# Two transformer stacks on one core: order of the first loads, of blocks at a seam, and of ScalarE's table loads

## Time and profile before

| what | value |
|---|---|
| three executions | 2781.55, 2787.64, 2789.39 us; median 2787.64 |
| the profiled execution | 2785.67 us |
| its span, first to last instruction | 2783.9 us |
| TensorE busy | 2505.9 us, 90% of the span |
| VectorE, ScalarE, GpSimd busy | 1736.6, 970.3, 672.7 us |
| DMA | 803.18 MB, 289 GB/s over the span |

### The profile page before, as it was taken

One profiled execution on the slowest core, in us unless ns is written; L12 is line 12 of the kernel. 1 busy time (PEld: TensorE's weight loads), 2 busy tenths in 40 slices (PEclk: granted clock), 3 DMA queues, 4 the chain that ended last, 5 costly groups with the idle time before them and its releaser, 6 DMA issues. The chain is left out here.

```text
span 2783.9 us, 29395 instructions
## 1 busy us (share of the span) xinstructions
PE 2505.9 (90%) x9829; PEld 1558.4 (56%) x9829; DVE 1736.6 (62%) x3951; ACT 970.3 (35%) x2012; POOL 672.7 (24%) x636
## 2 busy tenths in 40 slices
PE   8989888798887899887877799999999999999999
PEld 3544444364442465442322357885688668865787
DVE  1678766755758656667776456654565546646664
ACT  1225322234222353222221135442444445424543
POOL 0044433433434333444444211002000020002000
PEclk9999999999999999999999999999999999999999
DMA  8399999999999999999999832544154315533452
GB/s 336 116 408 421 416 421 421 414 421 417 406 421 419 406 394 372 421 421 422 421 421 421 356 123 103 198 153 180 49 208 166 143 71 193 185 118 121 148 188 102
DMA packets 112849, 803.18 MB, mean 289 GB/s; under 512 B 13139, under 2 KB 15782, under 8 KB 20310
## 3 DMA queue, kind: packets, MB, share of 16 engines
q0 software_dynamic: 74464, 540.07, 47.2%
q1 hardware_dynamic: 38262, 261.60, 24.8%
HBM read 800.55 MB, written 4.22 MB: 289 GB/s over the span
## 5 line engine op out<-in xcount | busy, mean ns | idle before, releaser
L1345 PE MATMUL psum<-weights,scratch 128*128 128x512 f32 x1232 | 587.6, 622 | 144.8 <-ACT scratch L1778 144.8
L2762 POOL DMA_INDIRECT weights<-in_peer_uv,scratch x308 | 355.7, 1155 | 593.4 <-PE psum L1345 496.7
L1345 PEld LDWEIGHTS psum<-weights,scratch 128*128 128x128 f32 x1232 | 232.3, 197 | 468.9 <-issue 244.4
L1345 PE MATMUL psum<-arena,scratch 128*128 128x512 f32 x816 | 388.1, 621 | 76.2 <-ACT scratch L1778 76.1
L2606 DVE TENSOR_TENSOR piece<-weights,piece 128x2048 fp32r<-128x2048 f32 x128 | 292.0, 2292 | 181.5 <-ACT piece L1857 181.5
L1076 PE MATMUL psum<-weights,xT 128*128 128x512 f32 (+2 forms) x792 | 340.2, 584 | 20.9 <-DMA weights<-in_w_qkv_a 12.2
L1453 PE MATMUL psum<-piece,hidden 128*128 128x512 f32 x1536 | 358.9, 390 | 0.0
L1770 ACT ACTIVATE scratch<-scratch 128x2 f32<-128x2 f32 x256 | 51.9, 203 | 844.6 <-DVE heads_arena L2257 843.8
L1410 PE MATMUL psum<-split_x,piece 128*128 128x512 f32 x896 | 318.6, 398 | 0.0
L1453 PEld LDWEIGHTS psum<-piece,hidden 128*128 128x128 f32 x1536 | 284.3, 188 | 59.6
L1345 PEld LDWEIGHTS psum<-arena,scratch 128*128 128x128 f32 x816 | 154.0, 196 | 287.4 <-issue 163.2
(11 more groups left out here) (264 smaller groups left out, 2762.6 us busy)
## 6 DMA issues: line engine op xcount, KB each, us to landing
weights<-in_w_up SPq DMA_DIRECT2D x64, 1024.0 KB, 4.9
weights<-in_w_down SPq DMA_DIRECT2D x64, 1024.0 KB, 4.9
weights<-in_w_kv_b SPq DMA_DIRECT2D x16, 1024.0 KB
weights<-in_peer_w_q SPq DMA_DIRECT2D x12, 1024.0 KB
weights<-in_a_w_in SPq DMA_DIRECT2D x6, 2048.0 KB, 8.8
weights<-in_w_q_b SPq DMA_DIRECT2D x8, 1024.0 KB
weights<-in_w_o_b SPq DMA_DIRECT2D x8, 1024.0 KB
weights<-in_a_w_out SPq DMA_DIRECT2D x4, 2048.0 KB, 8.4
```

The source lines that it names most:

```text
L1345: mm = pe.matmul(psum[g.bank][:, :], diagonal[:, n % DIAGONALS, :], row[:, D + half * BANK:D + (half + 1) * BANK], start=(k == 0), stop=(k ...
L2762: pool.indirect_dma_start(gathered[n % GATHER_SLOTS], None, rows, bass.IndirectOffsetOnAxis(ap=expert[:, w % NT, k:k + 1], axis=0), elemen ...
```

## The change

Seven edits, all in the order of the lists:

1. SyncE issues chunks 1 and 2, `const`, chunks 3, 4 and 5, and only then the small broadcasts and the tiny loads. lambda's broadcast gets a semaphore of its own, and `consts_loaded` counts the other eight.
2. `gain_turn` and the bias row move behind `later_blocks[2]` on TensorE, and their copies behind `diff_out_turn` on ScalarE; they use banks 6 and 7.
3. VectorE's waits move: for lambda alone ahead of its product, for the other eight ahead of `sublayer_norm(0)`, for `bias_read` ahead of `angles`, for `bias_written` ahead of the first window.
4. On ScalarE the sine goes ahead of the copy of the first expert queries.
5. In the seam's `selected`, tile 0 is multiplied with chunk 2 ahead of tile 1's turn.
6. `exp_ahead`, an exponential of one column whose result nothing uses, goes ahead of the copy of the last input block in `selected`.
7. The same in `window`.

```diff
--- before.py
+++ after.py
@@ -78,7 +78,7 @@
 PIECES = 2 * FF // PIECE_FF
 SPLIT_SLOTS = 4
 
-CONSTS_LOADED = 16 * 9
+CONSTS_LOADED = 16 * 8
 SBUF_START = 16512
 
 
@@ -375,6 +375,7 @@
         first_loaded = [sem(f"first_loaded{n}") for n in range(FIRST_PARTS)]
         const_loaded = sem("const_loaded")
         consts_loaded = sem("consts_loaded")
+        lambda_loaded = sem("lambda_loaded")
         values_loaded = [sem(f"values_loaded{n}") for n in range(2)]
         high_heads_loaded = sem("high_heads_loaded")
         bias_written = sem("bias_written")
@@ -708,8 +709,6 @@
 
         diff_in0 = in_ready.plan(2 * NT)
         diff_blocks = [diff_block(0, n, n) for n in range(4)]
-        gain_turn = Turn([([norm_gains[0:GAIN_ROWS, :]], gainT[:, 0:GAIN_ROWS].rearrange("p (a b) -> p a b", a=1))], (4,))
-        bias_row_group = group(5)
         diff_blocks.append(diff_block(0, 4, 6))
         diff_turn = diff_turned(0, (2, 3, 4, 5))
         diff_blocks.append(diff_block(0, 5, 7))
@@ -717,6 +716,8 @@
 
 
         later_blocks = {2: diff_block(1, 2, 0)}
+        gain_turn = Turn([([norm_gains[0:GAIN_ROWS, :]], gainT[:, 0:GAIN_ROWS].rearrange("p (a b) -> p a b", a=1))], (6,))
+        bias_row_group = group(7)
         diff_out_turn = maps_turned(0, (4, 5))
         diff_out_chunks = [halved_chunk(A["w_o_a"][0], 0, high_heads, high_heads_loaded, 16, None),
                            in_weights(A["w_o_a"][0], 1, 2, later_blocks[2][-1])]
@@ -930,9 +931,9 @@
 
         @block.sync
         def _(sp):
-            def load_small(name, src):
+            def load_small(name, src, loaded=consts_loaded):
                 at, width = SMALL_COLS[name]
-                sp.dma_start(small[:, at:at + width], src.partition_broadcast(P)).then_inc(consts_loaded, 16)
+                sp.dma_start(small[:, at:at + width], src.partition_broadcast(P)).then_inc(loaded, 16)
 
             def load_chunks(chunks):
                 for c in chunks:
@@ -972,10 +973,10 @@
                 part = slice(n * KB // FIRST_PARTS, (n + 1) * KB // FIRST_PARTS)
                 sp.dma_start(xT[:, part, :], A["x_turned"][:, part, :]).then_inc(first_loaded[n], 16)
                 sp.dma_start(first.view[:, part, :], first.src[:, part, :]).then_inc(first_loaded[n], 16)
-            load_chunks(diff_chunks[1:2])
+            load_chunks(diff_chunks[1:3])
             sp.dma_start(const[:, :], A["const"]).then_inc(const_loaded, 16)
-            load_chunks(diff_chunks[2:3])
-            load_small("lambda_qk", A["lambda_qk_a"][0].rearrange("a d -> (a d)"))
+            load_chunks(diff_chunks[3:6])
+            load_small("lambda_qk", A["lambda_qk_a"][0].rearrange("a d -> (a d)"), lambda_loaded)
             load_small("subln_g", A["subln_g_a"][0])
             load_small("a_q_gain", A["a_q_gain"].rearrange("a d -> (a d)"))
             load_small("a_k_gain", A["a_k_gain"].rearrange("a d -> (a d)"))
@@ -984,7 +985,6 @@
             load_small("b_sinks", A["b_sinks"][0])
             load_small("c_q_gain", A["c_q_gain"][0])
             load_small("c_k_gain", A["c_k_gain"][0])
-            load_chunks(diff_chunks[3:4])
             gain_at = 0
             for src, rows in ((A["norm_mix"], 4 * KB), (A["norm_mlp"], 4 * KB), (A["c_q_a_gain"], 2), (A["c_kv_a_gain"], 1)):
                 sp.dma_start(norm_gains[gain_at:gain_at + rows, :],
@@ -993,7 +993,6 @@
             sp.dma_start(pos_i[:, :], A["positions"][0].rearrange("(t p) -> p t", p=P),
                          allow_slow_non_contiguous=True).then_inc(bias_read, 16)
             sp.dma_start(rel_bias[0:N_BUCKETS, :], A["rel_bias"]).then_inc(bias_read, 16)
-            load_chunks(diff_chunks[4:6])
             load_chunks(diff_out_chunks[0:1])
             sp.dma_start(x[:, :, :], A["x"][0].rearrange("(t p) d -> p t d", p=P)).then_inc(x_loaded, 16)
             load_ln(0)
@@ -1493,8 +1492,10 @@
 
             def selected(l):
                 project(l.in0[1] if l.n == 0 else l.in0[0], turned=l.x_turn[0].done)
+                if l.n == 0:
+                    project(l.in0[2])
                 turn_normed(l.x_turn[1], l.normed0 + 1)
-                for n in range(2 if l.n == 0 else 1, 4):
+                for n in range(3 if l.n == 0 else 1, 4):
                     project(l.in0[n])
                 project(l.in1[2], turned=l.x_turn[1].done)
                 pe.wait_ge(prepared.sem, l.k_ready[0] + 1)
@@ -1573,12 +1574,6 @@
             project(diff_blocks[0:1], in_parts=True)
             project(diff_blocks[1:4])
             pe.wait_ge(const_loaded, 16)
-            pe.wait_ge(bias_read, 16 * 6)
-            turns(gain_turn)
-            bank_free(bias_row_group)
-            pe.matmul(psum[bias_row_group.bank][0:HEADS, 0:384], rel_bias[0:N_BUCKETS, :],
-                      const_at("bucket_of")[0:N_BUCKETS, :], start=True, stop=True)\
-                .then_inc(psum_filled[bias_row_group.bank], 1)
             project(diff_blocks[4:5])
             pe.wait_ge(in_ready.sem, diff_in0 + 1)
             turns(diff_turn)
@@ -1589,6 +1584,12 @@
                 copied(block[-1])
             attend(diff, "diff", 0, HEADS)
             project([later_blocks[2]])
+            pe.wait_ge(bias_read, 16 * 6)
+            turns(gain_turn)
+            bank_free(bias_row_group)
+            pe.matmul(psum[bias_row_group.bank][0:HEADS, 0:384], rel_bias[0:N_BUCKETS, :],
+                      const_at("bucket_of")[0:N_BUCKETS, :], start=True, stop=True)\
+                .then_inc(psum_filled[bias_row_group.bank], 1)
             pe.wait_ge(in_ready.sem, diff_in0 + 2)
             turns(diff_out_turn)
             project(diff_out_blocks, turned=diff_out_turn.done)
@@ -1629,6 +1630,10 @@
             def root(k, n, at=0):
                 act.wait_ge(root_asked.sem, k + 1)
                 act.activation(root_out[:, at:at + n], root_in[:, at:at + n], ACT.Sqrt).then_inc(root_given, 1)
+
+            def exp_ahead():
+
+                act.activation(lam[:, 6:7], lam[:, 5:6], ACT.Exp)
 
             def exps(att, sink0=None, first=0, last=NT * HEADS):
                 for u in range(first, last):
@@ -1789,9 +1794,9 @@
                 root(ln_root[0, 0], 1)
                 outputs([later_blocks[3]], to_y)
                 turns(peer_turn)
-                queries(0)
                 act.wait_ge(angle_ready, 1)
                 act.activation(ang[:, :, 2, 0:ROPE], ang[:, :, 1, 0:ROPE], ACT.Sin).then_inc(sine_ready, 1)
+                queries(0)
                 scores_of(peer_scores[0:2], 0)
                 gate(0, 0)
                 outputs([later_blocks[n] for n in (4, 5)], to_y)
@@ -1909,10 +1914,6 @@
                 return y[:, t, at:at + w]
 
             outputs(diff_blocks[0:4], to_y)
-            turns(gain_turn)
-            filled(bias_row_group)
-            act.activation(scratch[0:HEADS, 0:384], psum[bias_row_group.bank][0:HEADS, 0:384], ACT.Copy, scale=HD ** 0.5)\
-                .then_inc(psum_freed[bias_row_group.bank], 1)
             outputs(diff_blocks[4:5], to_y)
             turns(diff_turn)
             act.wait_ge(lambda_asked, 1)
@@ -1922,6 +1923,10 @@
             root(diff_root[0], PEER_HEADS)
             outputs([later_blocks[2]], to_y)
             turns(diff_out_turn)
+            turns(gain_turn)
+            filled(bias_row_group)
+            act.activation(scratch[0:HEADS, 0:384], psum[bias_row_group.bank][0:HEADS, 0:384], ACT.Copy, scale=HD ** 0.5)\
+                .then_inc(psum_freed[bias_row_group.bank], 1)
             first_queries()
             experts()
 
@@ -1943,6 +1948,7 @@
                 turns(l.key_turn[1], None, 0, -1)
                 keys_apart(l.key_turn[1].groups[-1], 1, 2, 1)
                 relus(l.index[1])
+                exp_ahead()
                 outputs(l.in1[1], to_y)
                 exps(l.att, None, 0, HEADS)
                 turns(l.out_turn[0])
@@ -2417,12 +2424,14 @@
                     for _ in steps:
                         pass
 
+                dve.wait_ge(consts_loaded, CONSTS_LOADED)
                 whole(sublayer_norm(0))
                 rope(later_blocks[2])
                 dve.wait_ge(x_loaded, 16)
                 add_to_x(diff_out_blocks, ALPHA)
                 whole(layer_norm(0, 0))
                 rope(later_blocks[3])
+                dve.wait_ge(bias_read, 16 * 6)
                 angles()
                 dve.tensor_tensor(small_at("c_k_gain")[:, 0:NOPE], small_at("c_k_gain")[:, 0:NOPE], small_at("c_q_gain")[:, 0:NOPE], ALU.mult)
                 then(dve.tensor_scalar(neg_sink[:, :], small_at("b_sinks"), -1.0, None, ALU.mult))
@@ -2430,6 +2439,7 @@
                 whole(route(0, 1))
                 shares(0, 0)
                 shares(0, 1)
+                dve.wait_ge(bias_written, 16)
                 second_norm = sublayer_norm(second.t)
                 for w in range(WINDOWS):
                     for pair in range(PAIRS_IN_TILE):
@@ -2660,7 +2670,7 @@
             for block in diff_blocks[0:3]:
```

(4 more changed lines are left out.)

## The result

The changed kernel took **2762.75 us** (median of 5 runs, 2758.80 to 2764.89) against 2787.64 (5 runs, 2778.89 to 2790.41), a ratio of **0.9924** (95% interval 0.9908 to 0.994). The forecast had the sign right and the size too small: a gain of 13.9 against 24.9 between the two medians, and 2773 with a range down to 2767. The five runs of before lay high: the two medians alone would give 0.9911, and in three later groups of 23 to 29 runs the kernel before had medians of 2782.38 to 2784.34. The profiled execution after took 2758.8, its span is 2757.0, TensorE's mean granted clock is 0.985 (before 0.981).

The account below looks back on a forecast made before the run. No engine bounds all: TensorE bounds start-up and the dense layers, with expert-row gathering near 420 GB/s between. Gains 6.9 + 0 + 4.1 + 2.9 = 13.9 us off the profiled 2785.67 gave 2771.8, as a median 2773; range 2767 to 2782.

Parts of the forecast that it names:

- part 1: Start-up: all projection chunks ahead of the small loads, so the fourth block ends earlier; 6.0 us, bounds 4.0 to 6.3.
- part 5: Exponential's table loaded ahead of selected and window attention in layers 0, 1 and 3; 0.96 us each, 2.9 in all.
- Part 2: Start-up: gain transpose and bias row moved behind attention; 0.9 us off TensorE, hidden later in a wait of 1.16.
- Part 3: Sine first on ScalarE, ahead of the first routing; worth 0 to 0.8 us, taken as 0.
- Part 4: Seam: tile 0's third block ahead of tile 1's transposes, key transposes at 1613.6 against 1617.75; 4.1 us, bounds 0 to 4.3.
- The two covers: Seam: third block's weights in by 1594.2 against 1595.9 needed; VectorE's keys ready by 1611.9, 1.7 us ahead of TensorE.
- A: Rival, start-up: bias copies meet the second output chunk's load, ending it up to 2.5 us late; 2776 us; chance 0.14.
- B: Rival: covers at the seam or early table loads fail; gain 6.9 + 0 to 3, 2779 us; chance 0.11.
- D: Rival: front gains nothing, chunk 3 held up in SyncE's queue; gain 7 to 8, 2780 us; chance 0.08.
- C: Rival: gathering of expert rows loses rate, 14 us per 1%; 2797 us at 1.7%; chance 0.05.
- Chance or linked: Experiments' two theories: 1.2 GHz stretches on TensorE come and go between executions, or follow waits the change removes.

Follow-up runs that it names:

- bridge13: Kernel before plus two dummy matmuls ahead of the fourteenth head's transpose in window attention's first tile, filling the wait of 1.26 us; ratio 0.9985.
- bridge_front: Kernel before plus eight dummy matmuls between the start's third and fourth blocks, in the wait for chunk 3; order of loads kept; ratio 0.9998.
- after_bridge13: Changed kernel plus two dummy matmuls ahead of the fourteenth head's transpose in window attention's first tile; 2764.15 us, ratio 0.9919 of the kernel before.
- the three parts alone: Three kernels, each the kernel before with only the front, only the seam or only the early exponentials changed; ratios 0.9963, 0.9983 and 0.9975.
- loads_only: Kernel before with only the new load order, its semaphores and VectorE's waits; gain turn and bias row stay between fourth and fifth block; ratio 1.0007.
- same_after: The changed kernel unchanged, run again for a second profile; 2764.37 us, ratio 0.9923 of the kernel before.
- bridge: Kernel before plus two dummy matmuls in selected and window attention, where TensorE waits for the first exponential behind the table load; ratio 0.9987.

## Why the prediction was wrong in size

The sum failed in two terms: 6.0 for part 1 (measured 47.5 - 38.2 = 9.3), where blocks two and three were priced at a row that held a slow stretch, and 2.9 for part 5 (measured 7.4), where three waits were priced by their length without the clock behind them. The account by stages, from means over the profiles of the table that had a part and those that had not:

| part | forecast | measured |
|---|---|---|
| front (parts 1 and 2) | 6.9 | 156.35 - 146.15 = **10.2** |
| sine | 0 | 0 |
| seam | 4.1 | 28.08 - 24.26 = **3.8** |
| table, layer 0 | 0.96 | **1.1** |
| table, layer 1 | 0.96 | 294.82 - 291.91 = **2.9** |
| table, layer 3 | 0.96 | 305.98 - 302.56 = **3.4** |
| sum | 13.9 | **21.4** |

The old front's 156.35 is the mean of six profiles (before to bridge13 in the table), 146.15 that of five. Layer 0's is the time from the key transposes to its long run of matmuls: 254.7 to 254.8 without the early exponential and 253.6 to 253.8 with it, three profiles with a stretch at 1.2 GHz there left aside (bridge13 and bridge_front, behind the table's wait, and after_bridge13). 21.4 is within 0.3 of what the ratio gives, and the three parts alone gave 10.3 + 4.7 + 7.0 = 22.0 by their ratios: the parts add up.

**Part 1 failed** in the term of 6.0 (6.3 at most). It set the new end of the fourth block at 40.3 and the old at 46.57. The new end is 38.2 (mean of five). 1.8 of the 2.1 between came from taking blocks two and three at the 15.70 of the earlier trace rows. That row held a stretch at 1.2 GHz behind the first wait; at full clock it is 13.9, and the row, though it says so by its own length, was carried into the new kernel. Only two of eight profiles with the old order of loads showed that slow pair; in the other six it took 15.0, with a wait of some 0.87 for chunk 2 in it, which the new order also removes. The remaining 0.9 is the profile's: its fourth block ended at 46.57, in six profiles of that front on average at 47.5, since chunk 3's arrival and the clock behind the wait vary. The forecast put the clock into its lower bound (4.0 "if the clock still costs something") and not into its upper one, where two blocks at full clock would have stood.

**Part 2** was right: 0.9 taken out, 0.35 of cover left. What it missed is that it is the condition of part 1, as loads_only shows.

**Part 3** was right.

**Part 4** was right in mechanism and nearly in size. The wait is worth 27.19 - 24.26 = 2.9 (means of the four profiles of the old seam with full clock and of five of the new); the clock adds 1.6 in five of nine profiles. The profiled one was of these, and 4.5 there stands against 4.1. The two covers held: no wait for weights but one of 0.29 in after_bridge13, none for the keys.

**Part 5 failed** in pricing three waits by their length alone. By length they were right: 1.1, 0.98 (291.95 - 290.97) and 1.04 (303.60 - 302.56), together 3.1 against 2.9. The other 4.3 are stretches at 1.2 GHz that follow. The earlier trace rows had shown the pattern and I priced it at the seam, but did not look at the stretch behind the same kind of wait in layers 1 and 3, where the earlier trace rows stopped at the first exponential. In layer 3 a stretch is behind the table's wait in six of nine profiles, and in none of five with that wait filled or removed. Two more of the nine have theirs ahead of it, so the change can't have taken that one away: in the first pair of profiles 1.65 of layer 3's 2.69 was such luck, and in the means some 0.4 of the 4.3. In layer 1 all eight profiles with both waits had the stretch, two of four with the table's wait alone removed or filled, none of two with the 1.26 filled. So it seems to need the wait of 1.26, and the early exponential to lower its chance; with four and two profiles neither is certain.

The Trainium skill, "TensorE: Matmul & The Clock Gate", section "HAM oscillation — how this bites in real kernels", ties the lower clock to pauses of TensorE between bursts, in its case waits for a DMA of some 3 to 5 us. The traces agree for the pauses of 4 to 9 at the start; in the layers and at the seam the clock also fell behind pauses of 0.9 to 2.8, shorter than those of that section, and there not every time. The skill's "ScalarE: Activation LUTs", section "What ACT_TABLE_LOAD costs", would give 8.0 for this part by a drain beside the load, an estimate by its figure. The measured 7.4 looks like it and is not: the load is 1.28, the wait it made is worth 1.0 to 1.1 each time, and the rest is TensorE's clock.

**The rivals.** A did not happen: the second output chunk is issued earlier with the front (78.19) and took 9.1 to landing, so it was in by 87.3, and the copies started at 87.74. The two did not meet, here or in same_after (85.2 and 85.67), so what a meeting would cost stays open. The small margin is no luck: in all six profiles in which the bias rows were written while the chunk was under way they landed 0.2 behind it (87.44 behind 87.27 in after), and the copies wait for them. B and D are out (seam and front in the table). C, the gathering: 1427.5 to 1434.0 over all profiles, a mean of 1430.6 in the eight with the old order of the loads and of 1430.5 in the five with the full new front. The change does nothing to it, and of the 26.9 between the two profiled executions 5.5 is this spread (1433.6 and 1428.0). It does not go by TensorE's clock: after and same_after took 1428.0 and 1433.6 at granted clocks of 0.97 and 0.98, with the DMA engines busy all the time (share 1.00) at 413 and 411 GB/s. What decides the rate was not tried.

**Chance or linked** ends between the two: at the start, the seam and in the layers each stretch at 1.2 GHz has a wait at or just ahead of it, and with that wait it comes in all profiles (the wait for chunk 3, seven of seven; layer 1 with both waits, eight of eight) or in some (seam, five of nine; the table's wait in layer 3, six of nine, in layer 0, two of nine).

## What to carry to other kernels

Price a wait of TensorE by its length and by the matmuls behind it: compare their duration with the same group elsewhere and read the granted clock of that stretch, in the row that you take a duration from as well. Here that was about 4 of 7.4 for three waits worth 1 us each. Two profiles of the same kernel do not settle what a stretch follows from: look in each where it begins, ahead of the wait or behind it. Before moving loads back, list their users: an order of loads and the order of their first users are one change, and half of it can be worth less than nothing. When a wait can't be removed, dummy matmuls can hold the clock, but they must be counted in time first: a 128x512 float32 one takes 0.9, and where they outlast the wait they can cost the difference (0.35 in bridge's layer 1).

## What the runs showed of the hardware

Behind a wait of TensorE of 1.26 in the middle of an attention of short matmuls the clock fell to 1.2 GHz in all eight profiles with both waits, at a cost of 2.9 to the layer; with that wait filled it did not (one profile, bridge13, and one of the changed kernel, after_bridge13). SyncE's issue of a DMA is held at the 18th DMA in both orders, for 6.7 to 7.5 in the eight profiles of the old and 8.0 to 8.4 in the six of the new, each time one of the small broadcasts; with the new order the five broadcasts behind it are held for 3.1 to 4.3 each. A chunk of 2 MB behind them waits with them: chunk 3 was issued at 23.33 before and at 6.85 after.
